# Squares of queries and keys in the dilated mixers: one fp32 sum, or two fp32r products of a high and a low part

## What is computed

```
def rms_norm(x, gain):
    xf = x.astype(jnp.float32)
    y = xf * lax.rsqrt(jnp.mean(xf * xf, axis=-1, keepdims=True) + EPS)
    return (y * gain.astype(jnp.float32)).astype(x.dtype)
...
def mixer_a(h, w_in, q_gain, k_gain, w_out, bias_tab):
    qkv = (h @ w_in).reshape(B, S, 3, A_N_GROUPS, A_HEADS, HEAD_DIM)
    q = rms_norm(qkv[:, :, 0], q_gain)
    k = rms_norm(qkv[:, :, 1], k_gain)
```

## Time and profile before

| | us |
|---|---|
| median of 3 runs | 2866.58 |
| lowest and highest | 2864.81, 2867.12 |
| the profiled execution | 2867.9 |
| its span | 2866.1 |

### The profile page before, as it was taken

One profiled execution on the slowest core, in us unless ns is written; L12 is line 12 of the kernel. 1 busy time (PEld: TensorE's weight loads), 2 busy tenths in 40 slices (PEclk: granted clock), 3 DMA queues, 4 the chain that ended last, 5 costly groups with the idle time before them and its releaser, 6 DMA issues.

```text
span 2866.1 us, 37354 instructions
## 1 busy us (share of the span) xinstructions
PE 2765.2 (96%) x14674; PEld 2207.0 (77%) x14674; DVE 1010.4 (35%) x1900; ACT 1093.6 (38%) x1641; POOL 1385.9 (48%) x1073
## 2 busy tenths in 40 slices
PE   7999999999989999999899997999999999999999
PEld 5977678888756788887677776888887977688887
DVE  3035422113485512224566663311223044522112
ACT  4355443223446422323334433422334355533221
POOL 3567544545455444445253442454445476554443
PEclk9999999999999999999999998999999999999999
DMA  4231123233422132223111110223323322123232
GB/s 123 89 88 52 45 89 103 88 102 91 100 44 75 59 103 96 95 93 106 45 45 45 41 49 16 88 89 103 102 88 96 95 67 67 45 89 99 91 102 73
DMA packets 271883, 227.81 MB, mean 79 GB/s; under 512 B 29204, under 2 KB 259348, under 8 KB 271748
## 3 DMA queue, kind: packets, MB, share of 16 engines
q1 hardware_dynamic: 260880, 216.29, 24.7%
q10 hardware_dynamic: 10868, 9.66, 1.5%
HBM read 223.62 MB, written 2.30 MB: 79 GB/s over the span
## 4 chain that ended last, share of the span: by engine, by line
PE 90%; DVE 5%; ACT 2%; POOL 1%; issue 1%; DMA 0%; ACTq 0%; DVEq 0%; POOLq 0%
PE bank L1765 49%; PE bank L1674 19%; PE bank L1826 5%; PE bank L2054 2%; PE bank L1801 2%; PE bank L2145 2%; PE bank L1719 1%; PE bank L1895 1%; PE bank L1879 1%; DVE arena L1459 1%; POOL w_lo L556 1%; PE bank L1863 1%; PE bank L2092 1%; PE bank L1856 1%; PE bank L1981 1%
## 5 line engine op out<-in xcount | busy, mean ns | idle before, releaser
L556 POOL TENSOR_TENSOR w_lo<-raw,w_hi 128x512 fp32r<-128x512 f32 x808 | 1073.7, 1358 | 1221.9 <-ACT w_hi L701 1221.9
L701 ACT ACTIVATE w_hi<-raw 128x2048 fp32r<-128x2048 f32 x202 | 385.4, 1908 | 456.9 <-PE bank L1765 423.3
L1765 PE MATMUL bank<-h_hi,w_hi 128*128 128x512 f32 x1024 | 400.8, 391 | 0.0
L1765 PE MATMUL bank<-h_hi,w_lo 128*128 128x512 f32 x1024 | 398.4, 389 | 0.0
L1765 PE MATMUL bank<-h_lo,w_hi 128*128 128x512 f32 x1024 | 398.4, 389 | 0.0
L1765 PE MATMUL bank<-g_hi,w_hi 128*128 128x512 f32 x1024 | 398.3, 389 | 0.0
L1765 PE MATMUL bank<-g_lo,w_hi 128*128 128x512 f32 x1024 | 398.3, 389 | 0.0
L1765 PE MATMUL bank<-g_hi,w_lo 128*128 128x512 f32 x1024 | 398.3, 389 | 0.0
L1674 PE MATMUL bank<-h_hi,w_hi 128*128 128x512 f32 x776 | 324.1, 418 | 7.2 <-POOL w_lo L556 7.2
L1674 PE MATMUL bank<-h_lo,w_hi 128*128 128x512 f32 x776 | 313.6, 404 | 0.0
L1674 PE MATMUL bank<-h_hi,w_lo 128*128 128x512 f32 x776 | 312.9, 403 | 0.0
(11 more groups left out here) (253 smaller groups left out, 3863.2 us busy)
## 6 DMA issues: line engine op xcount, KB each, us to landing
raw<-in_mlp_w SPq DMA_DIRECT2D x128, 1024.0 KB, 5.2
raw<-in_a_w_in SPq DMA_DIRECT2D x48, 512.0 KB, 5.1
raw<-in_c_w_in SPq DMA_DIRECT2D x32, 512.0 KB, 5.4
raw<-in_a_w_in SPq DMA_DIRECT2D x12, 1024.0 KB, 5.1
raw<-in_b_w_in SPq DMA_DIRECT2D x18, 256.0 KB, 4.2
raw<-in_a_w_out SPq DMA_DIRECT2D x4, 1024.0 KB, 4.9
raw<-in_b_w_in SPq DMA_DIRECT2D x4, 1024.0 KB, 5.5
arena<-bias_scratch ACTq DMA_DIRECT2D x16, 256.0 KB, 3.5
```

The source lines that it names most:

```text
L556: ins = nc.gpsimd.tensor_tensor(w_lo[s][:, k, :], raw[s][:, k, :], w_hi[s][:, k, :].bitcast(F32), ALU.subtract)
L701: nc.scalar.activation(w_hi[s][:], raw[s][:], ACT.Copy).then_inc(w_hi_done, 1)
L1765: mm = nc.tensor.matmul(lin_bank[j][:], w[s][:, c, P * j:P * j + P], a[:, c, :], start=c + z == 0, stop=c == CT - 1 and z == 2)
```

## The change

For the dilated mixers alone, the sum of a tile's squares is made of two fp32r products, as follows.

- ScalarE makes a rounded high part of `sq` with epsilon in it (`sq_high`), VectorE the rest as a low part (`sq_low`). Both go into columns 4 to 7 of `g_hi` and `g_lo`, four slots in turn (`sq_parts`); these hold nothing else in this mixer.
- TensorE multiplies each of them by `halves_r`, an fp32r copy of `halves` made by one activation at the start, and adds both in the bank.
- The next Square waits until the low part is there (`qlo_done`), not for the sum.
- In the first six tiles the sum of tile k-1 comes after the whole of tile k. In the filler the sum, the norm and the scaling of a tile come one share later (the tile of share G-2), and the parts are made in `part` of the share after its end. ScalarE's Square of a tile comes after the norm of an earlier tile where two end two shares apart (tiles 7 and 8, 16 and 17).

The new helpers (ScalarE, VectorE) and the sum (TensorE):

```
+            def sq_high(Q):
+
+                act.wait_ge(qsq_done, Q + 1)
+                if a_number[Q] >= 4:
+                    act.wait_ge(ssq_done, Q - 3 if a_number[Q] % (6 * A_PAIRS) >= 4 else Q)
+                nc.scalar.activation(sq_parts(Q)[0], mem[0]["sq"][0], ACT.Copy).then_inc(qhi_done, 1)
...
+            def sq_low(Q):
+
+                hi, lo = sq_parts(Q)
+                dve.wait_ge(qhi_done, a_number[Q] + 1)
+                nc.vector.tensor_tensor(lo, mem[0]["sq"][0], hi.bitcast(F32), ALU.subtract).then_inc(qlo_done, 1)
...
+                if kind == 0:
+                    hi, lo = sq_parts(Q)
+                    nc.tensor.matmul(stat_bank[:], halves_r[:], hi, start=True, stop=False)
+                    nc.tensor.matmul(stat_bank[:], halves_r[:], lo, start=False, stop=True).then_inc(ssq_done, 1)
+                    return
```

`part(G)` of ScalarE, then of VectorE, then the end of a share on TensorE:

```
                 def part(G):
+                    for k, n, t in a_ended(i, G - 2):
+                        qk_rms(0, a_q(i, k, n, t))
                     for k, n, t in a_ended(i, G - 1):
-                        qk_rms(0, a_q(i, k, n, t))
+                        sq_high(a_q(i, k, n, t))
                     for x in a_ended(i, G):
+                        qk(*x)
                         ended(*x)
```

```
                 def part(G):
+                    for k, n, t in a_ended(i, G - 1):
+                        sq_low(a_q(i, k, n, t))
                     for k, n, t in a_ended(i, G):
                         add_eps(0, a_q(i, k, n, t), ("query" if t == tile0[n] else "key", k % 3 > 0))
```

```
-                    for k, n, t in a_ended(i, G - 1):
+                    for k, n, t in a_ended(i, G - 2):
                         sum_qk(0, a_q(i, k, n, t))
...
-                    tile(n, t, 0, 12)
+                    tile(n, t, 0, 24)
                     sum_qk(0, Q + k - 1)
-                    tile(n, t, 12, 24)
```

More of the change, by code:

```diff
@@ L229, in trunk @@
             at_y += {0: A_PAIRS, 1: B_PAIRS, 2: C_HEADS}[KINDS[i]]
+        a_number = {}
         q_first, copy_first, at_q, at_c = {}, {}, 0, 0
@@ L233, in trunk @@
             q_first[i], copy_first[i] = at_q, at_c
+            if KINDS[i] == 0:
+                for k in range(6 * A_PAIRS):
+                    a_number[at_q + k] = len(a_number)
             at_q += {0: 6 * A_PAIRS, 1: 10, 2: 0}[KINDS[i]]
@@ L413, in a_near, with sq_parts @@
             return u % A_PAIR_UNITS < NB
+        def sq_parts(Q):
+            return g_hi[:, 4 + a_number[Q] % 4, :], g_lo[:, 4 + a_number[Q] % 4, :]
         def a_stat(f, k):
@@ L803, in qk_tile @@
                 sqs = mem[kind]["sq"]
-                if Q - q_base(kind) >= len(sqs) or (Q and len(sqs) == 1):
+                if kind == 0:
+                    if a_number[Q]:
+                        act.wait_ge(qlo_done, a_number[Q])
+                elif Q - q_base(kind) >= len(sqs):
                     act.wait_ge(ssq_done, Q - len(sqs) + 1)
@@ L847, in ended @@
                 def ended(k, n, t):
-                    qk(k, n, t)
                     if t + 1 == tile0[n + 1]:
@@ L883, in mixer_a @@
                 for k in range(6):
+                    n = chunk_at["aqk", i, k // 2]
+                    qk(k // 2, n, tile0[n] + k % 2)
                     if k:
                         qk_rms(0, Q + k - 1)
-                    n = chunk_at["aqk", i, k // 2]
+                    sq_high(Q + k)
                     ended(k // 2, n, tile0[n] + k % 2)
@@ L1292, in mixer_a @@
                     add_eps(0, Q + k, ("query" if k % 2 == 0 else "key", k >= 2))
+                    sq_low(Q + k)
                 for s in range(A_UNITS + 6):
@@ L1792, in sum_qk @@
             def sum_qk(kind, Q):
-                pe.wait_ge(qsq_done, Q + 1)
+                pe.wait_ge(qlo_done, a_number[Q] + 1) if kind == 0 else pe.wait_ge(qsq_done, Q + 1)
                 if Q:
```

3 lines of the change are left out of this document (added).

## The result

| | before | changed |
|---|---|---|
| median | 2866.51 (4 runs) | 2889.38 (4 runs) |
| lowest and highest | 2864.81, 2867.12 | 2888.91, 2891.40 |
| span of the profiled execution | 2866.1 | 2887.1 |

The change costs 22.9 us: ratio 1.0082, 95% interval 1.0067 to 1.0097. The forecast was 2866, its range ended at 2876.

What follows compares the result with a forecast made beforehand. TensorE, busy 96% of the span, was taken as the bound. Cheaper sums and removed waits against stalls at three places gave -0.4 us a layer, twice -0.8, so 2866 us; range for 8 in 10: 2852 to 2876.

Steps and rivals of the forecast that it cites:

- The three places: Steps 12 to 14, 17 to 20 and 25 to 29, without enough slack for the later copy: +1.35, +2.0, +3.9 us a layer.
- the two middle places: Steps 12 to 14 and 17 to 20: stalls of 2.2 and 4.0 us, net +1.35 and +2.0 a layer.
- first six tiles: Start of each dilated layer: 1.6 us of waits go and six cheaper sums save 2.5 us, -4.1.
- to step 13: Steps 1 to 8 -2.35 us from cheaper sums; steps 8 to 12 +0.45, with weigh of step 11 waiting for a copy.
- steps 17 to 20: Copy behind the mixing shifts by +2.5 us; weigh stalls 4.0 against 2.0 saved, net +2.0 a layer.
- steps 21 to 25: Filled part of each dilated layer: three cheaper sums, -1.25 us.
- the idle spot of step 26: TensorE idle before tile 17's sum until its low part ends: 5.4 us, 6.4 if POOL delays epsilon.
- the tail: Steps 25 to 29: late sum of tile 17 plus low clock on resuming, +2.55 to +6.55 us, taken as +3.9.
- the stall of steps 12 to 14: Square of tile 8 behind tile 7's norm, copy later by 0.57 + 2.06 us: 2.2 us of stall, net +1.35.
- 1.0 us each: In the slower rival (2874 us, chance 0.2): low part meets a POOL instruction at three places, at most 1.0 us each.
- the middle places were not covered: Faster rival was that they are covered: stalls of 2.2 and 4.0 us shrink or go, 2853 us; chance 0.3.
- the cold one: Slower rival: low clock from step 26 and the old slow stretch too, +6.55 instead of +3.9, 2874 us; chance 0.2.

Runs made afterwards that it cites:

- the experiment: Against the kernel before: the change in the first six tiles of each dilated mixer alone, filler keeping its fp32 sum and old order; 2855.3 us, ratio 0.9962.
- the order alone: The kernel before with the filler's sum, norm and scaling one share later, still one fp32 sum, no high and low parts; 2872.8 us, ratio 1.0025.
- Kept busy: The changed kernel with products whose result nobody reads put into TensorE's pauses in steps 13, 19, 20 and 26; 2878.0 us, ratio 1.0037.
- the cut splits: The changed kernel with GpSimd's splits of the filler's weights cut from 256 to 16 columns, low weights partly stale; 2870.4 us, ratio 1.0021.
- copy and high first: The changed kernel with VectorE's copy of turned weights directly behind the logits and ScalarE's high part ahead of the exps; 2859.3 us, ratio 0.9975.
- high part first: The changed kernel with second-share tiles' high part ahead of the next exps on ScalarE (step 26: ahead of the gate); 2865.3 us, ratio 0.9996.
- without the low part: The changed kernel without VectorE's 48 subtractions; TensorE adds the high part twice instead; 2863.5 us, ratio 0.9993.

## Why the prediction was wrong

The three places were right, and that VectorE's chain makes them. Two things failed in the sum, which had gains and stalls cancel: the stalls of the two middle places were priced too small, and the low clock behind these two was not priced at all. In the first mixer, by the steps of the prediction:

| | forecast | measured |
|---|---|---|
| first six tiles | -4.1 | -5.4, of it 0.4 before the first tile and 0.2 in its first products |
| to step 13 | -1.9 | -1.2 |
| steps 13 and 14 | +1.35 | +5.4 |
| steps 15 and 16 | -0.4 | +0.1 |
| steps 17 to 20 | +2.0 | +6.9 |
| steps 21 to 25 | -1.25 | +0.6 |
| from step 26 | +3.9 | +4.3 |
| sum | -0.4 | +10.8 |

**Right.** The sum as two records 0.23 us apart; no wait before the first sum, and a gain in the first six tiles (5.4 a mixer by the experiment, for 4.1; the waits in that sum are 1.46 + 0.6 - 0.3 = 1.8 and not 1.6, which changes little); the weigh of step 11 waiting for the copy (1.22 for 1.3); two differences waiting 0.78; the idle spot of step 26, 5.54 us in a forecast of 5.4 to 6.4, ended by the low part; the tail as a whole.

**Wrong, the stall of steps 12 to 14.** I had the copy 2.63 us later against weigh (0.57 for Square, 2.06 for the parts). It came 4.8 later: it ended 9.8 us after weigh of step 13, for 5.0 before. The 2.2 us between: epsilon started 1.16 us later against weigh instead of 0.57 (0.6); it took 1.83 instead of 2.12 (-0.3); L1307 took 1.79 instead of 0.68 (1.1), which I had not touched; and the low part took 1.49, not 0.69 (0.8). Weigh of step 14, for which I had a wait of 2 us, did not wait: the sum, which stands ahead of it, waited 3.66. More than half of the missing 2.2 us belongs to the order and not to the parts: with the order alone epsilon starts as late (1.89 us after weigh), and it and the instruction behind it take 1.83 and 1.79 us; I had given the order 0.57 us where it cost the copy 2.0. **Steps 17 to 20** the same: a stall of 1.6 and 4.0 where I had 4.0 in all, with 1.77 us for a mixing instruction that took 0.69.

I did name the meeting of the low part with GpSimd, as a rival, at "1.0 us each". The price was right, the count was not: I counted the low part alone, at three places a layer. In the changed kernel 22 of the 48 low parts ran beside a two-input instruction of GpSimd and took 1.35 us in the mean, for 0.69 of those beside nothing; most had the slack for it. A later epsilon meets another GpSimd instruction, and what follows on VectorE meets the next one, since both engines then take turns. The Trainium skill (SBUF — State Buffer, SBUF: two separate sides) says that a VectorE instruction with two SBUF inputs contends with a GpSimd instruction that reads SBUF, and that the one that starts second is blocked for the whole of the other. The trace agrees for GpSimd's two-input instructions: L1243 ends 0.54 us behind the split. Beside GpSimd's scaling of the weights, which reads one SBUF tensor and a column of scalars (L589), it does not, and the measurement decides: the low part at 216.70 took 0.84 us, 0.15 more than alone.

**Wrong, the clock.** I priced a stretch at 1.2 GHz behind the stall of step 26 and none behind the stalls of 13 and 20, though I forecast 2.2 and 4.0 us for them. Kept busy, the same kernel is 11.4 us faster, 5.7 a mixer; of this my 1.7 to 2.5 covered the tail alone. By the starts of the kernel kept busy, the clock was worth 2.3 us in steps 13 and 14 and 2.4 in 17 to 20. With 1.5 us more stall in the one place (3.66 for 2.2) and 1.6 in the other (1.60 and 4.03 for 4.0), the forecast's +1.35 becomes 5.1 of the 5.4 measured, and its +2.0 becomes 6.0 of 6.9.

Both terms point the same way, so their sum left the range. Neither rival happened as it was written. TensorE's waits between 220 and 300 us rose from 0.8 to 10.1, so the middle places were not covered; and near 320 us the clock was 0.59 from 324 to 330 and 0.98 from 330 to 336, so the tail was not the cold one. That the tail came out at 4.3 for 3.9 says little for its parts, whose ends lay 4 us apart. That the chain costs so much on an engine 37% busy was the point of the prediction; the cure was cheap and I had not looked for it: ScalarE stood idle 3.1 us before the exps of step 13 while the high part, whose input was ready at 222.67, stood behind them.

What stays open: where all of the 6.7 us of the order alone lie. Its traced execution is one of its shortest, 2869.7 us. From weigh of step 3 to that of step 34 its mixers take 4.7 us more than before, and 4.5 of them are waits; the rest is not located. Open too is how much of the 19 us of the cut splits is VectorE's meetings, and how much the freed GpSimd.

## To carry to other kernels

Here the added instructions cost their place, not their length: the same 48 subtractions and 48 roundings gave 2889 us behind the exps and 2852 with the rounding ahead of them, the copy that TensorE waits for ahead of the subtraction, and the Square ahead of the norm. Where a forecast has a pause of TensorE like the three here (3.7, 5.6 in two parts, 5.5 us), add the clock behind it at once, some 2 us each in these runs; and where it moves VectorE's two-input instructions, look at what GpSimd does at the new time for every one that is moved, not for the new one alone. A change of order moves instructions that it does not name: run it by itself before the parts are added.

## What was not expected of the hardware

- VectorE and GpSimd fall into turns: with two-input instructions on both sides, 0.68 us of work took up to 2.12 us on VectorE, and 1.3 us took 2.17 on GpSimd and once 2.80. Who gets in first is not fixed by the program, as the two mixers with copy and high first show. VectorE's copy from a bank is free of it. In the trace before, 12 of the copies (L1312) ran beside a two-input instruction of GpSimd and took 0.68 to 0.69 us each, and the changed kernel's groups have 0.68 in the mean of all 42:

```profile
L1346 DVE COPY arena<-bank 128x512 f32<-128x512 f32 x42 | 28.6, 681 | 0.1
```

- The same pause of 3.66 us was followed by a granted clock of 0.55 over six us in the first mixer and 0.72 in the second. A pause of 1.46 us (high part first, step 13) was followed by none that shows; one of 2.17 us (step 20 there) was followed by slow products (L1904, 1.23 us where 0.71 is usual) and a clock of 0.57 from 268 to 272 us, and one of 2.15 (without the low part, step 13) by 0.72 from 226 to 232. These runs give no length of pause at which it sets in.
